# A hybrid attention and gating step on one core: output inputs asked for ahead of stores, output weights split on two engines, a reordered opening

## What is computed

```python
u, va = gelu(h[u]), layernorm(gelu(h[va]))
a = u * (tril(w_sgu) @ va + b_sgu)            # per 128 rows, 4 groups
p = softmax(q @ k.T / 8 + rel_bias)           # band: 9 chunks of 64 keys, 8 heads
b = p @ v
y = concat(a * silu(za), b * silu(z))
out = layernorm(2**0.25 * x + y @ w_out) * ln_g + ln_b
```

## Time and profile before

| | us |
|---|---|
| median of 3 runs | 1073.99 (1073.51 to 1074.50) |
| the profiled execution | 1073.99 |
| its span, first to last instruction | 1071.9 |
| PE busy in the span | 1053.1 (98%) |
| DVE, ACT, POOL busy | 459.8, 353.0, 157.2 |

### The profile page before, as it was taken

How to read it: one execution, slowest core, us unless ns; L and a number is a source line. 1 busy time by engine, 2 the same in 40 slices (tenths; PEclk the granted TensorE clock), 3 DMA queues, 4 the chain that set the end, 5 groups by cost and what they waited for, 6 DMA issues and landing times.

```text
span 1071.9 us, 17673 instructions
## 1 busy us (share of the span) xinstructions
PE 1053.1 (98%) x7338; PEld 912.6 (85%) x7338; DVE 459.8 (43%) x944; ACT 353.0 (33%) x722; POOL 157.2 (15%) x160
## 2 busy tenths in 40 slices
PE   9999999999999999999999999999999999999995
PEld 7988889999999999999999887777888888888884
DVE  6545442212122111112112001877777777667654
ACT  6410011111111111111112112455666666666620
POOL 0011112020110000000000000742222222322211
PEclk9999999999999999999999999999999999999998
DMA  9561113222211233333331433765444543344112
GB/s 340 199 184 44 45 40 122 80 79 72 74 61 51 103 120 130 118 130 113 118 111 69 122 124 96 261 207 159 137 135 155 157 136 121 109 128 141 58 70 68
DMA packets 112287, 128.43 MB, mean 120 GB/s; under 512 B 7224, under 2 KB 86224, under 8 KB 112208
## 3 DMA queue, kind: packets, MB, share of 16 engines
q1 hardware_dynamic: 107312, 112.62, 32.6%
q10 hardware_dynamic: 4896, 14.68, 4.3%
HBM read 82.17 MB, written 48.26 MB: 122 GB/s over the span
## 4 chain that ended last, share of the span: by engine, by line
PE 97%; DVE 1%; DMA 1%; issue 0%; POOL 0%; POOLq 0%; ACT 0%; DVEq 0%; ACTq 0%; SPq 0%
PE s_ps L1228 35%; PE s_ps L1245 17%; PE out_ps L1430 16%; PE pt_ps L1228 8%; PE o_ps L1394 6%; PE s_ps L1323 6%; PE pt_ps L1365 3%; PE s_ps L1352 1%; PE s_ps L1430 1%; PE o_ps L1257 1%; PE out_ps L1257 1%; PE o_ps L1408 0%; PE out_ps L1264 0%; PE s_ps L1272 0%; DMA yr<-s_y 0%
## 5 line engine op out<-in xcount | busy, mean ns | idle before, releaser
L1228 PE MATMUL s_ps<-xh,ring 128*128 128x512 f32 (+1 forms) x1200 | 341.2, 362 | 0.8 <-ACT st L834 0.8
L1228 PEld LDWEIGHTS s_ps<-xh,ring 128*128 128x128 f32 x1200 | 221.2, 188 | 24.5 <-issue 1.2
L1228 PE MATMUL s_ps<-xl,ring 128*128 128x512 f32 (+1 forms) x600 | 217.1, 362 | 0.0
L1245 PE MATMUL s_ps<-ring,xh 128*128 128x512 f32 x544 | 169.8, 393 | 0.0
L1228 PEld LDWEIGHTS s_ps<-xl,ring 128*128 128x128 f32 x600 | 112.6, 188 | 11.9
L1245 PEld LDWEIGHTS s_ps<-ring,xh 128*128 128x128 f32 x544 | 100.5, 188 | 20.5 <-issue 0.3
L873 ACT ACTIVATE prob<-prob,low 128x640 f32<-128x640 f32 (+3 forms) x128 | 97.6, 764 | 57.5 <-DVE low L1078 57.5
L1078 DVE CUSTOM_DVE_ANT_1 prob<-s_ps,bias 128x640 f32<-128x640 f32 (+1 forms) x112 | 85.7, 803 | 54.5 <-PE s_ps L1323 54.3
L1430 PE MATMUL out_ps<-wo_h,yh 128*128 128x512 f32 x248 | 101.4, 409 | 4.8 <-DVE yl L1180 4.8
L1245 PE MATMUL s_ps<-ring,xl 128*128 128x512 f32 x272 | 106.0, 390 | 0.0
L1430 PE MATMUL out_ps<-wo_l,yh 128*128 128x512 f32 x248 | 98.3, 396 | 0.0
(11 more groups left out here) (151 smaller groups left out, 1225.1 us busy)
## 6 DMA issues: line engine op xcount, KB each, us to landing
raw<-w_all ACTq DMA_DIRECT2D x26, 512.0 KB, 3.6
r<-x SPq DMA_DIRECT2D x17, 512.0 KB, 3.8
q<-s_q SPq DMA_DIRECT2D x16, 512.0 KB, 4.2
k<-s_k SPq DMA_DIRECT2D x16, 512.0 KB, 6.0
y_out<-r SPq DMA_DIRECT2D x15, 512.0 KB, 2.7
x_raw<-x_t SPq DMA_DIRECT2D x12, 384.0 KB, 12.7
s_mix<-st SPq DMA_DIRECT2D x17, 256.0 KB, 2.3
v_all<-st SPq DMA_DIRECT2D x17, 256.0 KB, 2.0
```

Source lines behind the costliest of these rows:

```text
L1228: last = nc.tensor.matmul(bank[b][:, 0:width], w[:, kc, :], xx[:, kc, :], start=kc == 0 and a == 0, stop=kc == KC - 1 and a == 2)
L1245: last = nc.tensor.matmul(out, xx[:, kc, cols], ring[:, 0:GRP, side, kc, :], start=kc == 0 and a == 0, stop=kc == KC - 1 and a == 2)
```

## The change

Three parts:

1. SP: `load_y` of a cycle is issued ahead of that cycle's store, `load_x` and stream values. Its own wait (`out_done`, the tile two before is projected) stays.
2. w_out: ACT makes the high part of each piece (`high_wo`, in cycles 2 to 4), POOL makes only the low part, in two instructions of one k block each. `wo_done` counts k blocks.
3. The opening. The weights of z0 and z1 lie side by side in a new input `w_z` and come in five pieces (one, one, two, two, two k blocks, both groups in each). The first x piece is cut in two of 256 columns; DVE makes the high part of the first of them. ACT runs one small `Copy` after its first two DMA issues. The products that nobody reads are 8 instead of 9 and read a tile of ones that DVE writes, in place of the identity. PE goes through the first k block in two column halves, and in every k block multiplies both groups' high weights first, then both low ones.

```diff
-PIECES = [(0, k0, k0 + 1) for k0 in range(KC)] + [(c, k0, k0 + 2) for c in range(1, NCH) for k0 in range(0, KC, 2)]
+PIECES = [(0, 0, 1, 0, 256), (0, 0, 1, 256, 512)] + [(0, k0, k0 + 1, 0, 512) for k0 in range(1, KC)]
+PIECES += [(c, k0, k0 + 2, 0, CHUNKS[c][1]) for c in range(1, NCH) for k0 in range(0, KC, 2)]
+Z_PIECES = [(0, 1), (1, 2), (2, 4), (4, 6), (6, 8)]
-IDLE_PRODUCTS = 9
+IDLE_PRODUCTS = 8
...
 @block.sync
+                for n in range(TILES):
+                    if START[n] - 2 == cycle:
+                        if n == 0:
+                            sp.wait_ge(proj_done, DONE["v", 13])
+                        if n == 1:
+                            sp.wait_ge(proj_done, DONE["v", TILES - 1])
+                        load_y(n)
                 for n in range(TILES):
                     if STORE[n] == cycle and n < TILES - 2:
...
                     if b < SB - 1:
                         sp.wait_ge(s_weighed, b + 1)
                         load_values(b + 1)
-                for n in range(TILES):
-                    if START[n] - 2 == cycle:
...
-                        load_y(n)
...
 @block.gpsimd
-            def split_wo(j):
+            def low_wo(j):
                 h, k0 = j // 4, 2 * (j % 4)
-                held = (slice(None), slice(k0, k0 + 2), slice(None))
-                pool.wait_ge(wo_loaded[j], 16)
-                nc.gpsimd.tensor_copy(wo_h[h][held], wo_raw[h][held]).then_inc(wo_high, 1)
                 pool.wait_ge(wo_high, j + 1)
-                nc.gpsimd.tensor_tensor(wo_l[h][held], wo_raw[h][held], wo_h[h][held].bitcast(f32),
-                                        ALU.subtract).then_inc(wo_done, 1)
+                for kc in range(k0, k0 + 2):
+                    nc.gpsimd.tensor_tensor(wo_l[h][:, kc, :], wo_raw[h][:, kc, :], wo_h[h][:, kc, :].bitcast(f32),
+                                            ALU.subtract).then_inc(wo_done, 1)
...
 @block.scalar
-            for j in range(3):
-                for i in range(2):
-                    load_z_w(i, j)
-            for j in range(4):
-                for i in range(2):
-                    z_high(i, j)
-                    x_high(PIECES_OF[0][2 * j + i:2 * j + i + 1])
-                if j == 0:
-                    for i in range(2):
-                        load_z_w(i, 3)
+            load_z_w(0)
+            load_z_w(1)
+            act.wait_ge(const_ready, 2)
+            nc.scalar.activation(spare[:], eps[:], ACT.Copy)
+            load_z_w(2)
+            for j, (k0, k1) in enumerate(Z_PIECES):
+                z_high(j)
+                if j < 2:
+                    load_z_w(j + 3)
+                x_high([k + 1 for k in range(k0, k1)])
...
+            def high_wo(j):
+                h, k0 = j // 4, 2 * (j % 4)
+                held = (slice(None), slice(k0, k0 + 2), slice(None))
+                act.wait_ge(wo_loaded[j], 16)
+                nc.scalar.activation(wo_h[h][held], wo_raw[h][held], ACT.Copy).then_inc(wo_high, 1)
             for cycle in range(CYCLES):
                 copy_turned(2 * cycle - 2)
+                if cycle == V_CYCLES - 1:
+                    for j in (2, 3):
+                        high_wo(j)
                 for h in range(2):
                     exponent(2 * cycle, h)
+                if cycle == V_CYCLES:
+                    for j in (4, 5):
+                        high_wo(j)
...
                 copy_turned(2 * cycle - 1)
+                if cycle == V_CYCLES:
+                    for j in (6, 7):
+                        high_wo(j)
...
                     exponent(2 * cycle + 1, h)
+                if cycle == V_CYCLES - 2:
+                    for j in (0, 1):
+                        high_wo(j)
...
 @block.vector
-            for j in range(4):
-                for i in range(2):
-                    z_low(i, j)
-                x_low(PIECES_OF[0][2 * j:2 * j + 2])
+            nc.vector.memset(st[3][:, 0:P], 1.0).then_inc(warm_ready, 1)
+            _, held = piece(0)
+            dve.wait_ge(x_loaded[0], 16)
+            nc.vector.tensor_copy(xh[0][held], x_raw[0][held]).then_inc(xh_first, 1)
+            for j, (k0, k1) in enumerate(Z_PIECES):
+                z_low(j)
+                x_low([0, 1] if j == 0 else [k + 1 for k in range(k0, k1)])
...
 @block.tensor
-            pe.wait_ge(const_ready, 4)
+            pe.wait_ge(warm_ready, 1)
...
-                nc.tensor.matmul(out_ps[:, 0:P], ident[:], ident[:], start=True, stop=True)
-            for kc in range(KC):
-                pe.wait_ge(xh_done, PIECES_OF[0][kc] + 1)
...
+                nc.tensor.matmul(out_ps[:, 0:P], st[3][:, 0:P], st[3][:, 0:P], start=True, stop=True)
+            for m in PIECES_OF[0]:
+                _, kc, _, n0, n1 = PIECES[m]
...
+                for j in split:
+                    pe.wait_ge(z_w_high, j + 1)
                 for i in range(2):
...
+                    nc.tensor.matmul(bank[i][:, n0:n1], w_high(i)[:, kc, :], xh[0][:, kc, n0:n1], start=m == 0, stop=False)
+                for j in split:
+                    pe.wait_ge(z_w_split, j + 1)
                 for i in range(2):
...
+                    nc.tensor.matmul(bank[i][:, n0:n1], w_low(i)[:, kc, :], xh[0][:, kc, n0:n1], start=False, stop=False)
+                pe.wait_ge(x_split, m + 1)
...
                 if n == 0:
-                    pe.wait_ge(wo_done, 4 * h + c1 // 2)
+                    pe.wait_ge(wo_done, 8 * h + c1)
...
-        "w_all": c(w_all),
+        "w_z": c(np.stack([w_all[0], w_all[1]], axis=2)), "w_all": c(w_all[2:]),
```

82 lines of the change are left out of this document (42 added, 40 removed).

## The result

| | before | after |
|---|---|---|
| median of the runs, us | 1073.75 (1073.33 to 1074.50, 4 runs) | 1067.02 (1065.28 to 1068.84, 4 runs) |
| the profiled execution | 1073.99 | 1065.28 |
| its span | 1071.9 | 1063.3 |

The ratio is 0.9935, 95% interval 0.992 to 0.995: 6.7 us faster by the medians, 8.7 by the profiled executions. The forecast was 1063.2 with a range of 1060.4 to 1066.4, so the sign is right and the median lies 0.6 us above the range. Two more sets of runs of the same kernel, taken with the experiments, gave 1065.52 (1065.09 to 1067.92, 5 runs) and 1065.44 (1065.06 to 1066.84, 5 runs). Over all 14 runs the median is 1065.7, inside the range, and four of them lie above 1066.5. So two things have to be explained: 2.1 us that are missing even in the best runs, and runs that lie another 2 to 3.5 us higher.

What follows compares the result with a forecast made beforehand. PE is busy 98% of the span, so only its standstills and low-clock time could be won. The end 7.0, w_out split 3.1 and opening 0.7 sum to 10.8 us: 1073.99 to 1063.2, range 1060.4 to 1066.4.

Steps and rivals of the forecast that it cites:

- The end: Tile 16's y asked for ahead of the store: gap of 4.96 us and 2.0 of low clock go, 7.0 won.
- The cycles: Around the w_out split: 4.96 us of loss removed, less new stalls of 1.4 and 0.5, 3.1 won.
- The wait at unit 8: Cycles: PE waits for unit 7's bias, queued on DVE behind y's low part held by POOL; new stall of 1.4 us.
- The wait for the last half: Cycles: POOL's last half ends 7.3 us after `turn(7)` begins, PE wants it about 6.8 after; stall of 0.5.
- In all 4.96: Cycles: loss removed, PE waits of 1.21, 0.72 and 1.23 us plus 1.8 lost at the low clock.
- The opening: Earlier table load and first real matmul, limited by when x comes: 0.7 us won, bounds 1.3 and -0.3.
- What is late next is x. The fourth x block...: Opening: fourth x block lands at 8.5, its matmuls start at 11.02; with the change at about 10.3, 0.7 us won.
- the two queues may share evenly, x comes about a microsecond later: Opening: weights in 2 KB rows from the third piece on take DMA share from x, charged to its fourth block.
- the bound of -0.3: Opening's lower bound: one more x piece is issued ahead of the rest, 0.45 us on SP.
- Stalls traded: Rival, cycles: ACT's copies and the port keep as much as they free; gain 8.2, time 1065.8 us; chance 0.17.
- The opening gives nothing, because x comes later by what PE is early: Rival, opening: gain 10.1, or 9.8 with its lower bound, time 1064.2 us; chance 0.10.
- slower: Rival: ACT waits in order for late w_out pieces 4 to 7, holding transposes and exponents; 1076 at 22 us landing; chance 0.02.

Runs made afterwards that it cites:

- first run: Only load_y ahead of the stores, on the kernel before: 1066.61 us against 1074.35, ratio 0.9931.
- fifth: The changed kernel with the first block of x loaded whole (2 KB rows) instead of in column halves: 1065.11 us, ratio 0.9922.
- sixth: The changed kernel with its third, fourth and fifth weight pieces each asked for one step later: 1068.86 us, ratio 0.9955.
- third run: Only the opening (part 3) on the kernel before: 1073.90 us, ratio 0.9993; profiled in its longest run, 1076.27.
- eighth: The changed kernel again, unaltered, with a second profile: 1065.52 us, ratio 0.9928; the profiled execution took 1065.93.
- thirteenth run: The changed kernel with five more unread products between the first block of x and the second: 1065.88 us (1065.15 to 1066.04).
- tenth to twelfth runs: Three variants of the changed kernel with x's first block whole; the middle one has POOL's low parts whole instead of in halves: 1066.37 us, ratio 0.9929.
- tenth: The changed kernel with x's first block whole and ACT's copies 2 and 3 moved behind that cycle's second turn: 1064.07 us, ratio 0.9910.
- twelfth runs: The changed kernel with x's first block whole, copies 2 and 3 behind ACT's high part of y, ahead of the second turn: 1064.14 us, ratio 0.9910.
- seventh: Parts 1 and 2 with the old loads, plus only the early table load and early unread products of part 3: 1064.83 us, ratio 0.9921.
- fourth runs: Parts 1 and 2 with the old opening, on the kernel before: 1065.34 us, ratio 0.9919.
- run 256: Not a run number: the text reads "sixth run 256 KB of weights", a size in KB; the sixth run took 1068.86 us, ratio 0.9955.

## Why the forecast was right in sign and too low

The forecast was 10.8, and the profiled executions differ by 8.7: 0.2 more at the end, 1.15 less in the cycles, 1.2 less in the opening. The median of the first four runs lies another 1.7 us higher, by runs at a lower clock.

**The end: right.** 7.0 forecast, 7.2 in the profile, 7.7 by the medians of the first run, which holds 0.5 from the cycles. y was asked for at 1033.95 and ready at 1042.08, with 2.7 us of room where 2.4 was forecast, and the after-effect on the clock went with the gap.

**The cycles: right in mechanism, 3.1 forecast, 1.95 measured.** The wait at unit 8 came as worked out, 1.43 against 1.4, through y's low part held by POOL: 2.29, from 685.12 to 687.41, where the forecast has 684.5 to 686.8. The wait for the last half came at 0.68 against 0.5. A wait of 0.32 at unit 9 was not forecast. (That each scaling up to tile 0's projection was held is read too widely: the last two of cycle 3 take 0.35 and 0.36. No term rests on it.) Together the new waits are 2.43 instead of 1.9: 0.5 of the miss. The other 0.6 lies in the loss removed, which was put at 4.96, of which 1.8 was the clock's. The first run leaves the cycles as they were, and there the clock happens to stay at 1.00 over 700 to 730. PE in the second half of tile 0's projection, in the kernel before and then in the first run:

```profile
700.13 0.56 PE L1430 MATMUL out_ps<-wo_h,yh 128*128 128x512 f32 x1
707.38 0.59 PE L1365 MATMUL pt_ps<-ident,prob 64*128 64x64 f32 x12
...
699.99 0.50 PE L1430 MATMUL out_ps<-wo_h,yh 128*128 128x512 f32 x1
703.93 0.50 PE L1430 MATMUL out_ps<-wo_h,yh 128*128 128x512 f32 x1 [0.92 <-POOL wo_l L711]
706.90 0.59 PE L1365 MATMUL pt_ps<-ident,prob 64*128 64x64 f32 x12
```

The half takes 7.25 with the low clock in it and 6.91 without, so 0.34 is won: PE is sooner at POOL's last piece and waits 0.92 for it. All cycles of the first run take 51.76, only 0.47 less than the 52.23 with the clock down. So of the 1.8 us only 0.5 was to be won; the wait takes back most of the rest, and about 0.4 is not accounted for. From 51.76 to the changed kernel's 50.28 it is 1.48 us; the waits there were 1.8 + 1.2 + 0.9 = 3.9 and are 2.43: 1.5. So the sum closes: 1.3 less than charged for the clock, and 0.8 more for waits removed, 3.9 instead of 3.16. What failed is the step "In all 4.96": a stretch at the low clock was charged whole, 1.8, without asking what PE would wait for if it came sooner.

**The opening: wrong, +0.7 forecast, -0.47 measured in the profile.** The step that failed is "What is late next is x. The fourth x block...": I followed the fourth block, and the second is the one that is late. The share of the queues was rightly seen ("the two queues may share evenly, x comes about a microsecond later"), but it was charged to a block for which there is room, and not to the one which PE wants next after 1.7 us of work. And the bound of -0.3 was one issue on SP, 0.45; the 256 KB of weights ahead of that block on the other queue were not in it. The fifth and sixth runs show both: with one issue fewer and, by the estimate, 256 KB of weights fewer ahead of it the block lands 1.7 us sooner, and with the third weights asked for later it lands 1.2 sooner. The first matmul at 5.2 came at 5.31, the table load before 2 at 1.71.

**The runs that lie higher: not in the forecast.** The clock was charged for the stalls that the change removes, not for those that it leaves or makes. The wait in the opening cost 1.7 us beside itself in the third run's profile, the one at unit 8 0.9 us in the eighth's. That the highest runs of the changed kernel are longer by the clock is on record: the mean granted clock of the execution is 0.994 to 0.996 in the four of the 14 above 1066.5 (1066.84, 1067.89, 1067.92, 1068.84) and 0.996 to 0.999 in the others, and 0.001 of the span is 1.1 us. Behind which wait it fell in them wasn't seen, since none of them was profiled. For the opening's wait speak the thirteenth run, and the spreads: with the first block of x in halves and nothing in the wait five sets of runs spread over 1.8 to 4.3 us, with the block whole (fifth and tenth to twelfth runs) over 0.2 to 1.5. Against it: the sixth run, also in halves, spreads over 1.6 only, and the kernel before, with its old opening, over 1.7 to 6.3 us in its five sets of 9 to 19 runs. So the opening's wait isn't the only thing that moves the clock, and which wait makes the high runs stays open.

**The rivals.** "Stalls traded" is near the numbers, 1065.8 against medians of 1065.4 to 1067.0, but by luck: it has 0.5 from the cycles and 0.7 from the opening, where 1.95 and -0.47 were measured. "The opening gives nothing, because x comes later by what PE is early" had the mechanism, with too small a lower bound. Nothing of "slower" came: ACT's longest wait for a piece of w_out was 0.18 us.

**What could be kept.** The changed kernel with the first block of x whole and the copies 2 and 3 moved takes 1064.1 in both places tried (tenth and twelfth runs), ratio 0.9910 in each, against 0.9928 to 0.9935 of the changed kernel. The intervals overlap (up to 0.9926, and from 0.9916), so it is above all the spread, 0.2 to 0.55 us against 1.8 to 3.6, that speaks for it. Whether the new opening earns anything in it isn't shown: parts 1 and 2 with the old loads take 1064.8 to 1065.3 (seventh and fourth runs), the fifth run 1065.1, and the old opening with the copies moved was not run.

## What to carry to other kernels

When a load is moved or widened, follow each block in the order in which it is wanted, and count the bytes that both queues move ahead of it; the block to look at is the one that is wanted next, not the last. A stretch at the low clock is worth only what lies between it and the next wait: ask what PE meets if it comes sooner. And a wait that is left costs more than its length in some executions (1.44 us and then 0.9 more in the eighth run), so of two orders with the same best time, take the one that keeps PE at work.

## What the runs showed of the hardware that was not expected

- In the sixth run 256 KB of weights, asked for when seven pieces of x were on the other queue, took 7.4 us to land, against 3.9 for the 128 KB of the first piece.
- With five products that nobody reads, 1.28 us of work in a gap of 2.9, the granted clock was 1.00 behind the gap, where a wait of 2.29 without them had 0.85 and 0.73 behind it; one execution of each.
- The same wait, 1.43 and 1.44 us, had a granted clock of 1.00 behind it in one execution and 0.50 over 2 us in another.
- With POOL's subtractions one behind another DVE's scalings of 128x256 get in about once for each: they take 1.2 to 1.3 us against halves of 128x512, 2.3 to 2.4 against 128x1024, and 0.35 alone.
- In the changed opening the DMA engines move 105 GB/s in the mean over the first 4 us and 328 over the next 4; what makes a dip to 82 to 198 GB/s at 3.4 to 4.4 us, where the old opening moves 246 to 403, stays open.
